# A four-layer diffusion step: layer 1's modulation loads moved behind layer 0's experts, expert weights fetched as whole blocks

## What is computed

```python
for l in range(DEPTH):                       # 0 Fourier, 1 neighbourhood attention, 2 gMLP, 3 Mamba-2
    mp = adaln(c_ctx, ada_w[l], ada_b[l])    # silu(cond) @ w + b: six vectors of 1024 for each stream
    ms = adaln(c, ada_w[l], ada_b[l])
    ap = modulate(rmsnorm(hp, norm1_g[l]), mp, 0)
    a_s = modulate(rmsnorm(hs, norm1_g[l]), ms, 0)
    hp = hp + mp[:, 2] * mixer_l(ap);  hs = hs + ms[:, 2] * mixer_l(a_s)
    hp = hp + mp[:, 5] * hier_moe(modulate(rmsnorm(hp, norm2_g[l]), mp, 3), ...)
    hs = hs + ms[:, 5] * hier_moe(modulate(rmsnorm(hs, norm2_g[l]), ms, 3), ...)
```

## Time and profile before

| | |
|---|---|
| median of 3 runs | 1819.41 us |
| the profiled execution | 1819.15 us, its span 1817.4 us |
| PE busy | 1689.1 us (93%), in 8242 matmul records |
| DVE, ACT, POOL busy | 574.0, 368.7, 99.2 us |
| moved by DMA | 614.04 MB, mean 338 GB/s |
| chain that ended last | PE 67%, DMA 19%, DVE 5%, ACT 3%, SP's queue 2% |

### The profile page before, as it was taken

How to read it: one execution, slowest core, us unless ns; L and a number is a source line. 1 busy time by engine, 2 the same in 40 slices (tenths; PEclk the granted TensorE clock), 3 DMA queues, 4 the chain that set the end, 5 groups by cost and what they waited for, 6 DMA issues and landing times.

```text
span 1817.4 us, 20161 instructions
## 1 busy us (share of the span) xinstructions
PE 1689.1 (93%) x8242; PEld 848.4 (47%) x8242; DVE 574.0 (32%) x1321; ACT 368.7 (20%) x703; POOL 99.2 (5%) x151
## 2 busy tenths in 40 slices
PE   5999999989999999889999999989999999799994
PEld 2554333367455333334774433335786654433331
DVE  1142232220344233130022332314334992323223
ACT  2131010121233111021201211102222662211111
POOL 0000000000000000000000000000001850000000
PEclk8999999999899999999999999999999999899998
DMA  9999999999339999998644999999864575699993
GB/s 400 311 421 421 421 421 421 421 385 342 138 139 408 421 421 421 421 412 328 241 169 188 422 421 421 421 422 368 308 239 160 127 256 215 238 422 421 421 421 140
DMA packets 123151, 614.04 MB, mean 338 GB/s; under 512 B 16720, under 2 KB 16864, under 8 KB 60464
## 3 DMA queue, kind: packets, MB, share of 16 engines
q1 hardware_dynamic: 116112, 585.73, 80.2%
q0 software_dynamic: 6944, 26.96, 4.6%
HBM read 608.34 MB, written 4.33 MB: 337 GB/s over the span
## 4 chain that ended last, share of the span: by engine, by line
PE 67%; DMA 19%; DVE 5%; ACT 3%; SPq 2%; issue 2%; POOL 0%; DVEq 0%; POOLq 0%; ACTq 0%
PE psum L1108 17%; PE psum L603 14%; PE psum L596 12%; DMA ring<-in_moe_w_down 10%; PE psum L1144 9%; PE psum L1162 4%; PE psum L662 3%; DMA arena<-in_moe_w_down 3%; DMA acc<-in_moe_w_down 3%; SPq L429 1%; ACT arena L1501 1%; DMA ring<-in_na_w_qkv 1%; PE psum L1074 1%; PE psum L1091 1%; DMA ring<-in_fnet_w_o 1%
## 5 line engine op out<-in xcount | busy, mean ns | idle before, releaser
L1108 PE MATMUL psum<-ring,arena 128*64 128x512 f32 x1152 | 254.5, 594 | 0.0
L596 PE MATMUL psum<-at,ring 128*128 128x256 f32 x1024 | 223.6, 380 | 1.5 <-DMA ring<-in_na_w_qkv 1.5
L596 PEld LDWEIGHTS psum<-at,ring 128*128 128x128 f32 x1024 | 193.7, 190 | 30.0 <-issue 4.0
L603 PE MATMUL psum<-ring,at 128*128 128x512 f32 (+1 forms) x416 | 172.7, 570 | 0.4 <-DVE at L1819 0.4
L1108 PEld LDWEIGHTS psum<-ring,arena 128*64 128x64 f32 x1152 | 81.2, 137 | 157.6 <-issue 156.5
L1968 DVE TENSOR_TENSOR arena<-arena,psum 128x512 f32<-128x512 f32 x32 | 33.7, 1052 | 364.4 <-PE psum L1108 364.4
L1144 PE MATMUL psum<-ring,arena 128*64 128x512 f32 x624 | 141.4, 596 | 7.8 <-DMA ring<-in_moe_w_down 6.7
L1108 PE MATMUL psum<-arena 128*64 128x512 f32 x608 | 135.1, 594 | 0.5 <-DMA arena<-in_moe_w_up 0.5
L603 PE MATMUL psum<-ring,arena 128*128 128x512 f32 x288 | 128.1, 603 | 2.8 <-DMA ring<-in_fnet_w_o 2.8
L1162 PE MATMUL psum<-arena 128*128 128x512 f32 x256 | 118.4, 605 | 11.4 <-ACT arena L1501 9.0
L603 PEld LDWEIGHTS psum<-ring,at 128*128 128x128 f32 x416 | 75.4, 191 | 85.9 <-issue 83.5
(11 more groups left out here) (288 smaller groups left out, 1651.2 us busy)
## 6 DMA issues: line engine op xcount, KB each, us to landing
ring<-in_ada_w SPq DMA_DIRECT2D x43, 2048.0 KB, 13.6
ring<-in_moe_w_down SPq DMA_DIRECT2D x39, 2048.0 KB, 28.0
ring<-in_moe_w_up SPq DMA_DIRECT2D x38, 2048.0 KB, 20.6
ring<-in_moe_w_gate SPq DMA_DIRECT2D x34, 2048.0 KB, 20.7
arena<-in_moe_w_gate SPq DMA_DIRECT2D x22, 2048.0 KB, 23.1
arena<-in_moe_w_down SPq DMA_DIRECT2D x17, 2048.0 KB, 20.9
arena<-in_moe_w_up SPq DMA_DIRECT2D x16, 2048.0 KB, 27.0
ring<-in_ssd_w_in SPq DMA_DIRECT2D x12, 2048.0 KB, 10.4
```

The source lines that it names most:

```text
L596: last = nc.tensor.matmul(dst, slot(k)[:, c, m * P:(m + 1) * P], src[:, c, :], start=(c == 0), stop=(c == nk - 1))
L603: last = nc.tensor.matmul(dst, src[:, c0 + c, s * P:(s + 1) * P], slot(k)[:, wc0 + c, 0:cols], start=(start and c == 0), stop=(stop and c ...
L1108: last = nc.tensor.matmul(ps[b][e * CAP:(e + 1) * CAP, :], rows, slot_half(k, 4, e)[:, c, :], start=(h == 0 and c == 0), stop=(h == 1 and ...
```

## The change

Three things are changed.

1. **Order.** `A1.0.*` leaves layer 0: it is loaded and multiplied at the start of layer 1, three slots behind layer 0's last scatter and one between the transposes of the two streams, then turned (`ada_turned(1, 0)`), evicted and made into `modt`. All eight slots of layer 1's rounds 1 and 2 now stand behind Q0 to Q3, and its rounds are turned after Q2 and Q4. Layer 0 is issued as A0.0, O0, O1, A0.1, A0.2, experts; TensorE runs the Fourier units without slots between them, then stream 0 of O0, the four A0.1 slots, stream 0 of O1, stream 1 of O0, the four A0.2 slots, stream 1 of O1. Layer 0 then follows the stream-wise norm of the other layers.
2. **Router constants** are loaded in four long runs to `routers` in the arena and copied by DVE.
3. **Whole blocks.** `G5.0` is now all of expert 5 and `G5.1` all of expert 13 (runs of 16 KiB in place of 8 KiB; in the seventh room 8 KiB as before). TensorE waits for both blocks of a pair before its first product, and gives both back after its last. D7 alone keeps the two halves.

```diff
-    ada_names(0, (0, 1)) + ["O0", "A0.2.0", "A0.2.1", "O1", "A0.2.2", "A0.2.3"] + ada_names(1, (0,)),
-    mixed(1, [f"Q{j}" for j in range(6)]) + ["O0", "O1"] + ada_names(2, (0,)),
+    ada_names(0, (0, 1)) + ["O0"] + ada_names(0, (2,)) + ["O1"],
+    ada_names(1, (0,)) + mixed(1, [f"Q{j}" for j in range(6)]) + ["O0", "O1"] + ada_names(2, (0,)),
...
+    if n == 0:
+        return ada_names(0, (0,)) + ["O0", "O1"] + ada_names(0, (1, 2)) + MOE
...
-                    sp.dma_start(wr[:, :, :, EG:NR], a["wer"]).then_inc(consts_in, 16)
+                    sp.dma_start(routers[:, 0, 128:640], a["wer"].rearrange("p l c e -> p (l c e)")).then_inc(consts_in, 16)
...
-                        load(k, rooms[ROOM[k]].rearrange("p (e c n) -> p e c n", e=2, c=c), half)
+                        load(k, rooms[ROOM[k]].rearrange("p (c n) -> p c n", c=2 * c), rows[:, x + PAIRS * e, :, :])
...
+            def first_map():
+
+                map_part(0, 0, 0, 0, ft, 1)
+                for q in range(QUARTERS):
+                    ada_slot(0, f"A0.1.{q}")
+                map_part(0, 0, 1, 0, ft, 1)
+                ada_turned(0, 1)
+                map_part(0, 1, 0, 0, ft, 1)
+                for q in range(QUARTERS):
+                    ada_slot(0, f"A0.2.{q}")
+                stream_turned(0, 1, 0)
+                for half in range(2):
+                    last = dense_tok(AT[0, "O1"], 1, ps[out_bank(0, 1, 1)][:, :], ft, half * DC // 2, DC // 2,
+                                     half == 0, half == 1, wc0=half * DC // 2)
+                    if half == 0:
+                        ada_turned(0, 2)
+                last.then_inc(slot_done, 1)
...
                     stream_turned(n, which, s)
-                    if n and which == 0:
+                    if n == 1:
+                        if s == 0:
+                            ada_slot(1, "A1.0.3")
+                        else:
+                            ada_turned(1, 0)
+                    elif n and which == 0:
...
+                elif n == 1:
+                    for q in range(3):
+                        ada_slot(1, f"A1.0.{q}")
...
-                    for q in range(QUARTERS):
-                        ada_slot(n, f"A1.0.{q}")
...
+                    k = AT[n, f"{w}{x}.0"]
+                    arrive(k)
+                    arrive(k + 1)
                     for h in range(2):
-                        k = AT[n, f"{w}{x}.{h}"]
-                        arrive(k)
...
-                        last.then_inc(slot_done, 1)
+                    last.then_inc(slot_done, 2)
...
+                    k = AT[n, f"D{x}.0"]
+                    arrive(k)
+                    if x < LAST:
+                        arrive(k + 1)
                     for h in range(2):
-                        k = AT[n, f"D{x}.{h}"]
-                        arrive(k)
+                        if h and x == LAST:
+                            arrive(k + 1)
```

More of the change, by code:

```diff
@@ L69, in late_ada @@
     rest = ada_names(n, (1, 2))
-    return rest[:EARLY], {0: rest[EARLY:4], 1: rest[4:6], 2: rest[6:8]}
+    if n == 1:
+        return [], {0: rest[0:2], 1: rest[2:4], 2: rest[4:6], 3: rest[6:8]}
+    return rest[:3], {0: rest[3:4], 1: rest[4:6], 2: rest[6:8]}
+EVICTED = {1: {1: (1, 1), 3: (1, 2)}, 2: {0: (2, 1), 2: (2, 2)}, 3: {0: (3, 1), 2: (3, 2)}}
+TURNED = {1: {2: (1, 1), 4: (1, 2)}, 2: {1: (2, 1), 3: (2, 2)}, 3: {1: (3, 1), 3: (3, 2)}}
 def mixed(n, mains, lead=()):
@@ L96, with issued @@
 LAST = PAIRS - 1
[L99 to L112, removed]
+def issued(n):
+    if n == 0:
+        return ada_names(0, (0,)) + ["O0", "O1"] + ada_names(0, (1, 2)) + MOE
+    if n == 1:
+        return MIX[1][:-4] + ["A2.0.0", "A2.0.1", "G0.0", "G0.1", "A2.0.2", "A2.0.3"] + MOE[2:]
+    if n == 2:
+        return MIX[2][:-4] + ["G0.0", "G0.1"] + MIX[2][-4:] + MOE[2:]
+    return MIX[n] + MOE
+ISSUE = [AT[_n, _w] for _n in range(DEPTH) for _w in issued(_n)]
 assert sorted(ISSUE) == list(range(len(LOADS)))
@@ L134, in age @@
                 if b == RING + 2 and (n, b) not in entered:
-                    return {0: AT[0, "A1.0.0"], 1: AT[1, "A2.0.1"] if n == 1 else 0, 2: AT[2, "O3"], 3: AT[3, "O3"]}[n] + 0.5
+                    return AT[n, {0: "A0.2.3", 1: "A2.0.1", 2: "O3", 3: "O3"}[n]] + 0.5
                 return last.get(b, -1)
@@ L1019, in _ @@
                 if n == 0:
[L1020 to L1022 removed]
+                    pe.wait_ge(routers_ready, 1)
                     pe.wait_ge(fold_ready, 1)
[L1024 to L1029, removed]
[L1030 to L1045 removed]
+                stream_logits(n, 0)
+                if n in (1, 2):
+                    for q in range(2):
+                        ada_slot(n, f"A{n + 1}.0.{q}")
+                stream_folded(n, 0)
+                stream_turned(n, 1, 1)
+                stream_tokens(n, 0)
+                stream_logits(n, 1)
+                stream_folded(n, 1)
+                stream_tokens(n, 1)
+                if n in (1, 2):
+                    for q in range(2, QUARTERS):
+                        ada_slot(n, f"A{n + 1}.0.{q}")
                 pe.wait_ge(sel_ready, n + 1)
@@ L1269, in stream_stats @@
                 if t:
-                    act.wait_ge(h_ready, 8 * n + ((2 if n else 3, 4)[s] if which else (-2, 0)[s]))
+                    act.wait_ge(h_ready, 8 * n + ((2, 4)[s] if which else (-2, 0)[s]))
                 if s or t:
@@ L1462, in _ @@
                     y_root(1)
-                if n == 0:
-                    norm_stats(n, 1)
-                    ada_evicted(0, 2)
-                    norm_scaled(n, 1)
-                else:
-                    for s in range(S):
-                        stream_stats(n, 1, s)
-                        stream_scaled(n, 1, s)
-                    stream_tokens(n, 0)
+                for s in range(S):
+                    stream_stats(n, 1, s)
+                    if n == 0 and s == 0:
+                        ada_evicted(0, 2)
+                    stream_scaled(n, 1, s)
+                stream_tokens(n, 0)
                 for r in range(2):
```

95 lines of the change are left out of this document (43 added, 52 removed).

## The result

The changed kernel takes 1824.65 us (median of 20 runs) against 1820.1 us of the kernel before (20 runs): ratio 1.0022, interval 1.0013 to 1.0031. It is slower by a fifth of a per cent, 4 us. The forecast was no change at all, within a range of 1807 to 1832. The profiled execution took 1822.38 us with a span of 1820.6, 3.2 us longer than the span of before.

What follows compares the result with a forecast made beforehand. Transfers, saturated at 421 GB/s in the expert stages, were taken to bound the kernel, D6.1's landing ending each stage. Order -4.0, whole blocks +13.9 and faster packets -9.8 summed to +0.1 us: 1819.4 us, range 1807 to 1832.

Steps and rivals of the forecast that it cites:

- The last landing: End of each expert stage: the landing of D6.1, D6's second half, sets it; only PE work follows.
- D6's whole pair behind it: Layers 1 to 3: both D6 halves follow D6.1's landing, 3.5 us of PE each layer, 10.5 us in all.
- the line through 2 and 8 KiB packets: Expert transfers: packet cost extrapolated to 16 KiB gives 427 GB/s for 421, -9.8 us over 144 blocks.
- that estimate of 4.2 us: Expert transfers: the 16 KiB packets' gain by the skill's 3 cycles a packet, in place of 9.8 us.
- the low end of the range: Whole span: -9.8 - 6.7 + 2 for an early G0, written as about -12, giving 1807.
- an idle DMA: Layer 0 before the experts: DMA idle some 10 us until G0's two rooms come back near 134 us.
- One premise: Expert stages other than layer 3's start: later room returns cost nothing, some 20 us of transfers being queued.
- 127.0: Layer 0: time in us of the first expert product, with the whole pair given back 7.1 later, at 134.1.
- landing was put at 330: Layer 0: D6.1 lands near 330 us; the order alone put it at 332.3 in place of 347.96, -15.7 us.
- +40: Layer 1's start: Q0 starts 40 us after D6.1's landing, where it was 33.7; cost +6.3 us.
- +3 to +5, so 1823: Layer 1's start: rival that A1.0.3, turn and scaling serialise with a cold clock; chance 0.14, shared with small packet gain.
- The first release in layer 3: Layer 3's expert start: the first room comes back 3.4 us later while DMA stands idle, +3.4 us.

Runs made afterwards that it cites:

- d6_halves: The changed kernel with D6 as well as D7 in halves, all other expert blocks whole: 1814.13 us, ratio 0.9964 to the kernel before.
- the eight traces: Traces of the changed kernel and seven experiments with the same TensorE work up to layer 0's first expert product, which comes at 124.8 to 127.8 us.
- warm2: The changed kernel with unread filler products on TensorE, six before Q0 and two before each D6: 1818.72 us, ratio 0.9986 to the kernel before.
- d6_warm: The changed kernel with D6 also in halves and six filler products before Q0, none before D6: 1812.46 us, ratio 0.9956 to the kernel before.
- order_only: The changed kernel with all expert blocks in halves again, new order and router constants kept: 1815.83 us, ratio 0.9969 to the kernel before.
- blocks_only: The kernel before with whole expert blocks alone, its order, constants and layer 1 unchanged: 1827.8 us, ratio 1.0042 to the kernel before.
- best: The changed kernel with A1.0 back in layer 0 and D6, D7 and pair 0's gate blocks in halves: 1808.76 us, ratio 0.9923 to the kernel before.
- a1_in_0: The changed kernel with A1.0 back in layer 0 and three round 1 blocks ahead of Q0, blocks whole: 1822.23 us, ratio 1.0007 to the kernel before.
- d6g0_halves: The changed kernel with D6, D7 and pair 0's gate blocks in halves, A1.0 still in layer 1: 1811.12 us, ratio 0.9952 to the kernel before.
- g0_halves: The changed kernel with pair 0's gate blocks as well as D7 in halves, D6 whole: 1818.62 us, ratio 0.9991 to the kernel before.

## Why the prediction was wrong

**The mechanisms stand.** The last landing sets the end of each expert stage; D6's whole pair behind it is the largest cost: 10.5 us were summed for it, and d6_halves gains 10.6 by the ratios, though that takes in the low clock at D6 too (3.2 us, below), so the 10.5 are not confirmed to size. With 16 KiB packets the windows show 427 GB/s, the forecast figure, from the line through 2 and 8 KiB packets (37.9 ns for 1 KiB, where the prediction writes 37). The exact hit is partly luck, since the line rests on a stretch at 389 GB/s whose neighbour had 370, and since the seventh room's blocks still come in 8 KiB packets. By the rule of the Trainium skill, "DMA: Bandwidth & Descriptors", section "Why small descriptors are slow", some 3 cycles for each packet, the estimate was 0.6%; the windows show 1.4%, and the measurement decides. (With that estimate of 4.2 us the sum is +5.7, not the +5.9 written; the low end of the range, added up as written, is -14.5 and not -12. Neither touches the outcome.) Layer 0 went as told: an idle DMA from about 123 to 132 us, the first room back 7.1 us after the first product (125.15 to 132.27), in layer 3 also (1571.88 to 1579.01). One premise was false and cost nothing that shows: the queue does run dry at the end of layer 1 (144 GB/s from 775 to 780 us, where before had 421), but no product of layer 2's mixer waits for a transfer.

**Layer 0 gained 2.5 us more in this trace.** The first product of the experts came at 125.15, where 127.0 was taken, and D6 started at 327.54, where landing was put at 330. Of this 1.9 us lie before the first product, and 0.6 between the first release (132.27) and D6, 195.3 us against the forecast 195.9. The 1.9 us lie within scatter: the middle of the eight traces is 127.2, so the 127.0 was right.

**Layer 1's start lost 2.2 us more before Q0.** The scaling into `at` (2.9 us) began at 363.71 and so ended at 366.6, 39.1 us after D6's start, as summed. But Q0 itself landed late. SP could issue it at 353.94, when the first A1.0 slot was counted off, and it ran beside the last A1.0 block, POOL's three tables and two blocks of round 1 issued right behind it (355.66 to 357.74); PE went on at 369.69, 42.2 us after D6's start, where +40 was taken. These two errors cancel, which is why Q0 starts on the forecast to 0.2 us.

**The step that failed** is the sum's silence on TensorE's clock behind a wait. The 40 us of layer 1's start were taken as a delay alone, and Q0's 14.05 us as fixed. The wait of 6.46 us that the change makes there brought the clock to its lower level, and Q0 took 17.07: +3.0 us. That the clock, and not the order or the blocks by some other way, turns the sign is shown by warm2: fillers alone take the ratio from 1.0022 (1.0013 to 1.0031) to 0.9986 (0.9974 to 0.9998). The prediction had this as a rival ("+3 to +5, so 1823") and gave it, with another, 0.14. The row that should have raised it was there: 0.70 from 1560 to 1577 us, where PE is busy 12.7 of 17 us; the prediction used it for layer 0's stretch and not for Q0.

**D6's clock is the same omission.** In layers 1 and 3 the first piece took 5.35 and 5.11 us in place of 3.65: +1.7 and +1.5. With Q0's that makes 6.2 us which no term held. warm2, which takes away some 1.3 of the first and both of the others, 4.5 in all, gained 2.3 us by the spans and 6.5 by the ratios: the clock's cost at these places together is shown, its size to within that, and how it divides between Q0 and D6 is not.

**What went the other way.** The sum missed by +3.1 us by the spans (about 4.4 by the medians of 20 runs), not 6.2. Some of the rest is in the trace of before, which had losses of its own that after doesn't have and that no term covers. In layer 3 PE stood 1.02 us ahead of D7, with nothing to wait for:

```profile
1786.55 7.09 PE L1144 MATMUL psum<-ring,arena 128*64 128x512 f32 x32 [1.02 <-issue]
```

And the clock of before sagged where that of after didn't: the mean of the granted clock from 1245 to 1255 us and from 1412 to 1422 us is 0.83 in both stretches, against 1.00 in after.

**The first release in layer 3** was put at +3.4 us. The trace of layer 3 with it undone says 1.3, so the term may be up to 2.1 too large; the ratios (2.2 and 5.6 us, with layer 0's in them) don't settle it. How the 6.2 us of clock become 3.1 at the end is therefore not shown. Part of Q0's 3.0 may be absorbed on the way: d6_warm, which restores Q0's clock, kept 0.6 to 1.5 us of it at the end.

**Where the gain went.** A change worth some 14 us and costing as much was forecast near zero, and terms of 3 us then decide the sign. order_only shows the gain that was there (0.3%), blocks_only the cost (0.4%), and best that both ideas were sound: what did not pay was whole blocks at one place, D6, and A1.0 at one place, ahead of Q0, where TensorE has nothing else to do (for A1.0 the runs say so less firmly: 2.7 us in a1_in_0, 5 in best).

## What to carry to other kernels

Make transfers coarse only where many are queued; the last one before a dependence should be fine, so that half of the work is done when it lands: one pair of eight decided 0.6% of the time here. Where an edit puts a wait in front of products, price the products behind it at the lower clock too, and look whether some real work (here, the next layer's modulation) can fill the gap. A sum that is the difference of two large terms needs its small terms all the more.

## What the runs showed of the hardware

- 8 KiB packets move 421 GB/s in the expert windows; with 16 KiB ones in all rooms but the seventh it is 427, at the same DMA share of 1.01.
- TensorE's clock: after 6.46 us without work Q0's 64 records took 17.07 us, after 6.98 us 15.97 (d6g0_halves), after 5.37 us 16.77 in d6_halves and 15.44 in order_only, after 3.43 us 16.95 (g0_halves), after a gap shortened to 1.94 us 15.74, with none 14.05. After 2.60 and 2.61 us, D6's first piece took 5.35 and 5.11 us in place of 3.65. So the length of the gap does not settle it: in a1_in_0 D6 of layer 3 had waited 2.60 us and took 3.65, and in blocks_only D6 of layer 0 had waited 3.27 us and took 3.65. What makes the difference is open.

```profile
1773.76 3.65 PE L1145 MATMUL psum<-ring,arena 128*64 128x512 f32 x16 [2.60 <-DMA ring<-in_moe_w_down]
```

- Work added in gaps can cost next to nothing: with four slots (7.1 us) between router and positions the granted clock from 110 to 120 us is 1.00 instead of 0.50, and the experts start at 122.8 and 126.1 us in two traces, against 124.8 to 127.8 in eight without them.
- A float filler product of 128 x 512 costs 0.9 us (six took 5.40), so fillers have to be sized to the gap: some 2 us too many at each D6, and 9 ahead of Q0, made it 0.5% slower than with none.
